# Latent attention's norms, projections and rotations moved into the last tile of a recurrence

## The reference, cut to what matters

```python
y_c = rwkv7_time_mix(pc, mu, ...)            # state recurrence, 8 heads of 64
def latent_attention(q_down, kv_down, k_rope, positions, q_norm, w_uq, kv_norm, w_ukv):
    q = (rmsnorm(q_down, q_norm) @ w_uq).reshape(b, L, 8, 64 + 32)
    kv = (rmsnorm(kv_down, kv_norm) @ w_ukv).reshape(b, L, 8, 64 + 64)
    q_nope, q_pe = q[..., :64], rope(q[..., 64:], positions)
    k_nope, v = kv[..., :64], kv[..., 64:]
    k_pe = rope(k_rope[:, :, None, :], positions)[:, :, 0]
    ... # per head: softmax(scale * (q_nope k_nope + q_pe k_pe), masked by chunk) @ v
x = x + jnp.concatenate([y_c, y_d], axis=-1) @ w_out
```

## Time and profile before

| | |
|---|---|
| median of 3 runs | 2590.21 us (2586.98 to 2597.19) |
| profiled execution | 2589.24 us; its span 2587.5 us |
| mean granted TensorE clock | 0.947 |
| busy: TensorE, VectorE, ScalarE, GpSimd | 90%, 46%, 36%, 5% of the span |
| the last tile's first transposes to its last product | 1041.5 to 1093.8 us of the span |
| latent projections, to the first scores | 1102.75 to 1160.58 us |
| first product with V | 1177.93 us |

### The profile page before, as it was taken

One profiled execution on the slowest core, in us unless ns is written; L12 is line 12 of the kernel. 1 busy time (PEld: TensorE's weight loads), 2 busy tenths in 40 slices (PEclk: granted clock), 3 DMA queues, 4 the chain that ended last, 5 costly groups with the idle time before them and its releaser, 6 DMA issues.

```text
span 2587.5 us, 41374 instructions
## 1 busy us (share of the span) xinstructions
PE 2328.5 (90%) x17025; PEld 2057.6 (80%) x17025; DVE 1197.8 (46%) x1602; ACT 927.3 (36%) x1180; POOL 119.6 (5%) x182
## 2 busy tenths in 40 slices
PE   7987799999989777678949999999999999999995
PEld 6863688888878666645949898989889999999995
DVE  3265443323253666635248888888878100000001
ACT  4346232222232333225326766666767000000001
POOL 6001000000000000000000000000010100000000
PEclk9988899999989888889959999999999999999998
DMA  6310222242222000010169999999999877777763
GB/s 181 120 66 1 66 82 93 87 134 90 90 82 62 2 2 2 2 49 17 36 209 344 340 346 346 344 343 332 343 340 325 284 258 235 267 260 246 235 221 118
DMA packets 334014, 452.44 MB, mean 175 GB/s; under 512 B 8391, under 2 KB 291886, under 8 KB 333710
## 3 DMA queue, kind: packets, MB, share of 16 engines
q1 hardware_dynamic: 328896, 435.73, 50.2%
q0 software_dynamic: 4752, 14.00, 2.2%
q10 hardware_dynamic: 190, 0.05, 0.0%
HBM read 437.22 MB, written 12.52 MB: 174 GB/s over the span
## 4 chain that ended last, share of the span: by engine, by line
PE 83%; DVE 8%; ACT 5%; issue 3%; DMA 1%; ACTq 0%; DVEq 0%; POOLq 0%; SPq 0%; POOL 0%
PE bank L664 80%; PE bank L667 4%; DVE arena L1861 2%; DVE slot L1861 1%; DVE w_low L1861 1%; ACT w_high L1778 1%; ACT arena L1545 0%; ACT w_high L1400 0%; DVE h_mix L1861 0%; DVE small L1914 0%; DVE arena L2048 0%; ACT slot L1554 0%; DMA arena<-h_rows_d,idx_ahead 0%; DMA xs<-sum_rows_d 0%; ACT arena L1432 0%
## 5 line engine op out<-in xcount | busy, mean ns | idle before, releaser
L1861 DVE TENSOR_TENSOR w_low<-slot,w_high 128x2048 fp32r<-128x2048 f32 x172 | 393.5, 2291 | 313.7 <-ACT w_high L1400 265.4
L664 PE MATMUL bank<-arena 128*128 128x144 f32 (+8 forms) x2672 | 371.1, 306 | 14.3 <-DVE arena L1861 7.9
L664 PEld LDWEIGHTS bank<-arena 128*128 128x128 f32 (+4 forms) x2672 | 318.0, 184 | 42.9 <-issue 21.7
L664 PE MATMUL bank<-w_high,xg_high 128*128 128x256 f32 x1120 | 324.6, 290 | 11.8 <-issue 5.4
L664 PE MATMUL bank<-w_low,xg_high 128*128 128x256 f32 x1120 | 317.1, 283 | 0.0
L664 PE MATMUL bank<-w_high,xg_low 128*128 128x256 f32 x1120 | 316.5, 283 | 0.0
L664 PE MATMUL bank<-arena,slot 128*128 128x144 f32 (+3 forms) x2304 | 298.0, 309 | 19.4 <-ACT slot L1695 14.8
L1861 DVE TENSOR_TENSOR arena<-arena,bank 128x256 f32<-128x256 f32 (+3 forms) x134 | 63.9, 477 | 529.8 <-PE bank L664 529.8
L664 PEld LDWEIGHTS bank<-arena,slot 128*128 128x128 f32 (+2 forms) x2304 | 284.0, 192 | 30.2 <-ACT slot L1695 15.8
L1861 DVE TENSOR_TENSOR w_low<-arena,w_high 128x2048 fp32r<-128x2048 f32 x105 | 240.6, 2291 | 53.3 <-ACT w_high L1778 53.3
L1778 ACT ACTIVATE w_high<-slot 128x2048 fp32r<-128x2048 f32 x108 | 206.9, 1917 | 78.8 <-PE bank L664 49.8
(11 more groups left out here) (358 smaller groups left out, 3390.0 us busy)
## 6 DMA issues: line engine op xcount, KB each, us to landing
slot<-in_moe_w_gate_dram SPq DMA_DIRECT2D x64, 1024.0 KB, 6.0
arena<-in_moe_w_down_dram SPq DMA_DIRECT2D x64, 1024.0 KB
slot<-in_moe_w_up_dram SPq DMA_DIRECT2D x56, 1024.0 KB, 6.6
arena<-in_moe_w_up_dram SPq DMA_DIRECT2D x56, 1024.0 KB, 6.4
arena<-in_moe_w_gate_dram SPq DMA_DIRECT2D x48, 1024.0 KB
slot<-in_moe_w_down_dram SPq DMA_DIRECT2D x48, 1024.0 KB, 6.5
slot<-in_e_w_in_dram SPq DMA_DIRECT2D x12, 1024.0 KB, 6.4
slot<-in_ff_w_gate_dram SPq DMA_DIRECT2D x11, 1024.0 KB, 5.3
```

The costliest lines, as they stand in the source:

```text
L664: return pe.matmul(o, lhsT, rhs, start=start, stop=True, skip_group_check=True)
L1861: return dve.tensor_tensor(o, a, b, op)
```

## The change

- *Norms.* The squares of all four tiles are made in tiles 0 and 1; means (`latent_means`) and root in t = 2; the scaling of rows (`latent_norm`) in t = 2 (two tiles) and in t = 3 after n = 0 (two).
- *Angles* in three pieces after n = 0, 1, 2 of t = 3; the two Sin on ScalarE after n = 3.
- *Transposed rows* in t = 3 after n = 0, five banks by feature block instead of eight by token; ScalarE copies and scales them.
- *Queries*: two tiles after each of n = 1 to 4. *Values*: two tiles after the z and u products, two between the chunks; ScalarE copies them, not VectorE. *Keys* after the last chunk; then the rotary keys' transposes, then `outputs_by_feature(3)`.
- *Rotations*: keys and heads 0 to 3 after n = 4 of t = 3, heads 4 to 7 right after. TensorE waits for each half ahead of its heads' transposes.
- *Attention*: the four `high_odd` at i = 2, 4, 6, 8 and two `high_dense` at i = 13, 17 on ScalarE, `low_odd` at i = 4, 6, 8, 10 and `low_dense` at i = 15, 19 on VectorE.
- *Places* of `qT_d`, `kT_d`, `v_d`, `kvnT`, `rope_cs` in the arena.

The diff, cut. The bodies of the new functions on TensorE are those of the removed loops.

```diff
@@ regions
-        qT_d = region(18064, HEADS, SEQ, rows=QD)
-        kT_d = region(22160, HEADS, SEQ, rows=QD)
-        v_d = region(11264, NT, C_WIDTH)
+        qT_d = region(22160, HEADS, SEQ, rows=QD)
+        kT_d = region(11264, HEADS, SEQ, rows=QD)
+        v_d = region(18064, NT, C_WIDTH)
...
@@ _(pe)
+                def latent_rows():
+                    pe.wait_ge(sem("qkvn_ready"), NT)
+                    for k in range(5):
+                        b, former = tile("qnT_ready", k + 1)
+                        pe.wait_ge(*former)
+                        for t in range(NT):
+                            m = tp(b[:, P * t:P * (t + 1)], qkvr[:, t, P * k:P * (k + 1)])
+                        m.then_inc(sem("qnT_full"), 1)
...
+                        if t == NT - 1 and upto >= 5:
+                            if n == 0:
+                                latent_rows()
+                            else:
+                                queries(2 * n - 2)
+                                queries(2 * n - 1)
...
+                    if t == NT - 1 and upto >= 5:
+                        values(0)
+                        values(1)
...
+                        if t == NT - 1 and c == 0 and upto >= 5:
+                            values(2)
+                            values(3)
+                if upto >= 5:
+                    for h in range(HEADS):
+                        keys(h)
+                    pe.wait_ge(sem("rope_ready"), 1)
...
                 outputs_by_feature(NT - 1)
@@ _(act), attention
+                    if i in (2, 4, 6, 8):
+                        high_odd(i // 2 - 1)
+                    if i in (13, 17):
+                        high_dense(phase_splits(O_OUT)[0] + i // 17)
@@ _(act), recurrence
-                        if n == 3:
+                        if n == 3 and t < 2:
                             act.wait_ge(sem("qkvr_stored"), total("qkvr_stored", 12))
...
+                            for u in (2 * t, 2 * t + 1):
...
+                        if t == 2 and n == 4:
+                            act.wait_ge(sem("mla_ms"), 1)
+                            act.activation(small[:, 168:176], small[:, 160:168], ACT.Sqrt).then_inc(sem("mla_rstd"), 1)
+                        if t == NT - 1 and upto >= 5:
+                            if n == 0:
+                                latent_rows()
+                            else:
+                                queries(2 * n - 2)
+                                queries(2 * n - 1)
+                            if n == 3:
+                                act.wait_ge(sem("angle_ready"), 1)
+                                for i in range(2):
+                                    act.activation(rope_cs[:, 4 * i:4 * i + 4, :], rope_cs[:, 4 * i:4 * i + 4, :], ACT.Sin).then_inc(sem("sin_ready"), 1)
...
@@ _(dve), attention
+                    if i in (4, 6, 8, 10):
+                        low_odd(i // 2 - 2)
+                    if i in (15, 19):
+                        low_dense(phase_splits(O_OUT)[0] + i // 19)
@@ _(dve), recurrence
-                        if t == NT - 1 and n == 0:
-                            rope_angles()
-                    if t == NT - 1:
-                        latent_norms()
+                        if upto >= 5:
+                            if t == 2 and n == 3:
+                                latent_means()
+                            if t == 2 and n == 4:
+                                latent_norm(0)
+                                latent_norm(1)
+                            if t == NT - 1 and n == 0:
+                                latent_norm(2)
+                                latent_norm(3)
+                            if t == NT - 1 and n < 3:
+                                rope_angles(n)
+                            if t == NT - 1 and n == 4:
+                                rope_keys()
+                                rope_queries(0)
+                    if t == NT - 1 and upto >= 5:
+                        rope_queries(1)
```

More of the change, by code:

```diff
@@ L1138, in _ @@
                         m.then_inc(sem("yc_full"), 1)
+                        if t == NT - 1 and c == 0 and upto >= 5:
[5 more added lines that the diff above has]
+                    pe.wait_ge(sem("rope_ready"), 1)
+                    b, former = tile("kpe_ready", 1)
+                    pe.wait_ge(*former)
+                    for t in range(NT):
+                        m = tp(b[0:QD, P * t:P * (t + 1)], qkvr[:, t, QKVR - QD:QKVR])
+                    m.then_inc(sem("kpe_full"), 1)
@@ L1139, in _ @@
                 outputs_by_feature(NT - 1)
             if upto >= 5:
[L1143 to L1160, removed]
@@ L1170, in _ @@
[L1170 to L1176 removed]
+                for h in range(HEADS):
+                    if h % 4 == 0:
+                        pe.wait_ge(sem("rope_ready"), 2 + h // 4)
                     b, former = tile("qT_ready", h + 1)
@@ L2153, in latent_norms @@
-                def latent_norms():
+                    if piece == 0:
+                        for i in range(16):
+                            step(dve.memset(small[:, 16 + i:17 + i], ROPE_THETA ** (-i / 16)))
+                        step(dve.tensor_copy(small[:, 252:256], small_i[:, 0:NT]))
+                    if piece == 1:
+                        step(dve.tensor_copy(ang, small[:, 16:32].unsqueeze(1).to_broadcast([P, NT, 16])))
+                        step(tt(ang, ang, small[:, 252:256].unsqueeze(2).to_broadcast([P, NT, 16]), ALU.mult))
+                        step(dve.tensor_scalar(turns, ang, 1.0 / (2 * math.pi), MAGIC, ALU.mult, ALU.add))
+                        step(dve.tensor_scalar(turns, turns, -MAGIC, None, ALU.add))
+                        for part in TWO_PI:
+                            step(dve.scalar_tensor_tensor(out=ang, in0=turns, scalar=-part, in1=ang, op0=ALU.mult, op1=ALU.add))
@@ L2154, in latent_norms, with latent_means @@
+                    if piece == 2:
+                        step(dve.tensor_scalar(ang, ang, 3.1415925, -3.1415925, ALU.min, ALU.max))
+                        step(dve.scalar_tensor_tensor(out=turns, in0=ang, scalar=-1.0, in1=ang, op0=ALU.mult, op1=ALU.max))
+                        dve.tensor_scalar(turns, turns, -1.0, math.pi / 2, ALU.mult, ALU.add).then_inc(sem("angle_ready"), 1)
+                def latent_means():
                     dve.wait_ge(sem("mla_ss"), 1)
```

163 lines of the change are left out of this document (82 added, 81 removed).

## The result

The changed kernel takes 2570.83 us in the median of 5 runs (2567.66 to 2573.78), against 2590.21 (2582.53 to 2597.19): a ratio of 0.9927, with a 95% interval of 0.9903 to 0.9951, or 19.4 us less (13 to 25). 2568 was forecast. A second series gave 2571.61 and 0.9930 (0.9909 to 0.9951). The profiled execution took 2570.7 us.

The account below looks back on a forecast made before the run. TensorE was taken as the bound, so only its idle time, or work whose results are not yet wanted, could give time back. 23.5 - 41.05 - 9.35 + 5.0 = -21.9 us gave 2568, range 2558 to 2580.

Parts of the forecast that it names:

- Norms and squares: Squares in tiles 0 and 1, norms in t = 2: cost 0, hidden while ScalarE and VectorE wait; 2.5 us without cover.
- Tile: Last tile of the recurrence, with transposed rows, queries and values put in: its products end 23.5 us later.
- cold spell: Rival, chance 0.10: a new wait in n = 0 drops TensorE's clock; 3 to 4 us a spell, 2572 to 2575.
- The Sin wait: After n = 3, ScalarE's Sin table load and two Sin precede the copies for n = 4, uncovered: +1.7 us.
- Recurrence's end to first score: From the recurrence's last product to the first attention score: 25.7 us instead of 66.75, so -41.05.
- ScalarE's copies pace them at 0.86: Query heads' transposes before the first score: ScalarE's copies set 0.86 us a head, 5.4 us in all.
- First score to first product with V: First head of attention, splits no longer ahead of it: 8.0 us instead of 17.35, so -9.35.
- Pieces in attention: High parts, low parts and weight splits moved into the attention loop, with small change: +5.0 us, bounds 0 and +12.9.
- Attention pays in full: Rival, chance 0.12: the pieces moved into attention cost their whole length in series; 7.9 us more, 2576.
- The filled stretch runs at the lower clock: Rival, chance 0.02: about 60 us of work, from the transposed rows to the keys, runs at 1.2 GHz; near 2628.

Follow-up runs that it names:

- norms_early: Changed kernel with all four row norms scaled in t = 2 instead of two there and two in t = 3; one execution took 2561.18 us.
- kpe_early: Changed kernel with the rotary keys' transposes ahead of the last two heads' keys and VectorE's copy not waiting for y; first score 5.7 us earlier.
- after: The changed kernel itself, all parts of the change against the kernel before; 2570.83 us in the median, ratio 0.9927.
- exp_ahead: Changed kernel with one small unused exponential on ScalarE ahead of the attention; first score to first product with V 8.11 us instead of 9.01.
- dense_at: Changed kernel with weight splits at i = 15, 23 and their low parts at 19, 27; first to last product with V 54.69 us instead of 57.18.
- all_late: Changed kernel with norms in t = 2 and the rest of the latent part after the recurrence's last product; 2558.98 us, ratio 0.9894.
- sin_late: Changed kernel with the Sin table and two Sin moved behind the copies that step n = 4 needs; first score 2.27 us earlier.
- gaps: all_late with row transposes ahead of the last tile's own and two query tiles ahead of its inversion; first score at 81.81 us, 9.5 earlier.
- splits_back: Changed kernel with high and low parts and the two weight splits back ahead of the attention loop; 2572.52 us, ratio 0.9947 to the kernel before.
- splits_only: Kernel before with only the high and low parts and two weight splits moved into the attention loop; 2585.48 us, ratio 0.9991.

## Why the prediction was right, point by point

**The total**: -21.9 forecast, -19.4 in the medians, -17.5 and -19.8 in the stages of two traces. The mechanism was the one named: the group norm, the rotations and the splits no longer stand between products. That the total came so close is in part luck: the tile and the first head were 3.2 us worse than forecast together, and the pieces in attention 2.2 us better. From the mark the first score came 15.0 us earlier (17.6 forecast), the first product with V 23.3 (27 forecast).

**Norms and squares cost 0 in tiles 0 to 2**: from the first tile's first pair product to the last tile's it was 181.72 us before and 181.69 after. The two norms left in t = 3 did cost 2.35 us of waiting in n = 0, as worked out (TensorE restarts 17.55 us after the mark; 17.64 forecast).

**Tile: +23.5, measured +25.7.** The term mis-sized is the work between 1065.85 and the z products. The transposes took 3.45 us instead of 2.4 and step 1 3.78 instead of 3.3, since the lower clock of n = 0 lasted into them (granted 0.76 from 1063.0 to 1070.2); I had priced them at full clock and kept the cold spell as a rival of 0.10. norms_early bears the reason out for the transposes (2.47 us without the wait) but for step 1 it can't: there it is 3.79 again, with a wait of 0.63 us for ScalarE in it. Both traces of the changed kernel have it. A pair of query tiles took 4.07 us from start to start instead of 3.88. The Sin wait was 1.58 for 1.7; values, z products and chunks 20.1 us for 19.8.

**Recurrence's end to first score: -41.05, measured -40.7.** Right in size. The reason given for one part was wrong: "ScalarE's copies pace them at 0.86". kpe_early shows 0.50 a head for ScalarE; what took 0.86 in after was TensorE transposing at half clock (granted 0.50) behind its wait for the rotary copy. In the kernel before the grant was 0.67 there (1156.0 to 1160.6).

**First score to first product with V: -9.35, measured -8.3.** I let the Exp table load run during the scores, as it had run before a wait in the kernel before. It started after the first maximum. exp_ahead gets 0.9 of the missing 1.0 back.

**Pieces in attention: +5.0, measured +2.8.** A weight split cost 1.22, not 1.8; low and high parts cost 0.04, not 0.5 at two places; another 0.35 is the low clock in the last head. A split of 1.93 us that costs 1.22 found 0.7 of slack, more than ScalarE's idle 0.47 in the earlier trace rows. dense_at shows that nearly all of the splits' cost was the place.

**Rivals.** "Attention pays in full" fell (2.8 of 12.9). "The filled stretch runs at the lower clock" fell: it ran at 1.00 from the first query tile to the keys. "Cold spell" came true in small, 1.5 us in the tile, and at another place (after the last head) in a size that changes from one execution to the next. On the 2.66 us that the Trainium skill (ScalarE: Activation LUTs, What ACT_TABLE_LOAD costs) gives for a change of table: the Sin in after starts 1.29 us after its load started. In exp_ahead the load (1143.55) starts 0.02 us after the copy ahead of it has ended, so no drain stands before it either. TensorE's wait was 1.58. The traces stay against the page.

**What I did not ask** was whether the filled tile was the right place. The prediction costed the fill at nearly its full length, which was right, and that implies what all_late then showed: the fill could as well stand after the last product.

## What to carry to other kernels

Before moving independent work into a busy stage, list the waits of the bound engine that are longer than a piece of it: only there is it free. Here the 4.7 and 3.8 us before the pair products and the inversion gave 9.5 us (0.8 of it not surely theirs), while pieces between back-to-back steps gave none. In strict queues place a piece where its own engine waits *and* no result for the bound engine stands right behind it; two and six steps further along in the loop 1.22 us became 0.16.

## What the runs showed of the hardware

- A wait of a few us can cost more than its length. Behind a wait of 3.82 us the low clock lasted over 5.39 us of products that take 3.34 at full clock. Behind one of 4.27 us 24 transposes took 5.35 us in after and 4.49 in sin_late, where 32 take 3.67 at full clock: the price of the same wait varies. Behind 2.12 us, in gaps, the grant was 1.00. The Trainium skill (TensorE: Matmul & The Clock Gate, HAM oscillation — how this bites in real kernels) warns of re-throttling after idle gaps; the trace agrees, 0.78 against 1.00 granted with the gaps filled.
- An ACT_TABLE_LOAD does not always run ahead in ScalarE's idle time. In the kernel before, and in splits_back, the Exp load started right behind the weight splits, 3.1 us ahead of the exponential, which then waited 1.78 us for the first maximum. In after, splits_only and all_late, with the splits gone from there, ScalarE was idle for 1.16 us and the load came only after the first maximum. An exponential of its own ahead of the attention, in exp_ahead, brought 0.9 us of the load's 1.28 off the path. A reading that fits the program order is that the load takes over semaphore waits of the activation behind it, more of them where no other instruction has taken them before; no run shows that directly.
